# A decoder trunk on one core: the feed-forward layers' products go from rows of two into alternation of wide and narrow

## What is computed

```python
def conv_ffn(h, w_up, conv_w, conv_b, w_down):
    u = jnp.einsum('bsd,df->bsf', h, w_up)          # 2048 -> 11264
    S = u.shape[1]
    y = conv_b
    for tap in range(CONV_WIDTH):                   # 3
        shifted = jnp.pad(u, ((0, 0), (tap, 0), (0, 0)))[:, :S]
        y = y + shifted * conv_w[CONV_WIDTH - 1 - tap]
    val, gate = jnp.split(y, 2, axis=-1)
    return jnp.einsum('bsf,fd->bsd', jax.nn.silu(gate) * val, w_down)   # 5632 -> 2048

for l in range(DEPTH):                              # 2
    ...
    h = rms_norm(x, ffn_norm[l])
    x = x + conv_ffn(h, w_up[l], conv_w[l], conv_b[l], w_down[l]).astype(x.dtype)
```

## Time and profile before

| | |
|---|---|
| median of 3 runs | 1958.37 us (1958.27 to 1959.3) |
| the profiled execution's own time | 1958.57 us |
| its span, first to last instruction | 1956.4 us |
| TensorE busy | 1939.8 us (99%), 11078 products |
| VectorE, ScalarE busy | 1391.3 us (71%), 1110.1 us (57%) |
| granted TensorE clock | 0.998 of full |

### The profile page before, as it was taken

How to read it: one execution, slowest core, us unless ns; L and a number is a source line. 1 busy time by engine, 2 the same in 40 slices (tenths; PEclk the granted TensorE clock), 3 DMA queues, 4 the chain that set the end, 5 groups by cost and what they waited for, 6 DMA issues and landing times.

```text
span 1956.4 us, 31302 instructions
## 1 busy us (share of the span) xinstructions
PE 1939.8 (99%) x11078; PEld 1690.7 (86%) x11078; DVE 1391.3 (71%) x2152; ACT 1110.1 (57%) x1845; POOL 48.2 (2%) x53
## 2 busy tenths in 40 slices
PE   8999999999999999999999999999999999999998
PEld 8888888888888888888888888888888888888887
DVE  6667776767777777777655557877777777755554
ACT  6555554556665665665555456665665566545554
POOL 0002240000000000000000000000000000000000
PEclk9999999999999999999999999999999999999999
DMA  9654545555555555554565555555555555555653
GB/s 324 194 172 154 185 158 172 192 182 186 194 191 183 185 192 193 185 183 168 194 213 183 186 171 179 188 193 188 183 187 192 193 183 184 191 177 184 204 188 108
DMA packets 205202, 364.91 MB, mean 187 GB/s; under 512 B 6563, under 2 KB 49100, under 8 KB 205132
## 3 DMA queue, kind: packets, MB, share of 16 engines
q1 hardware_dynamic: 203388, 362.34, 55.9%
q10 hardware_dynamic: 1744, 1.63, 0.3%
HBM read 361.83 MB, written 2.11 MB: 186 GB/s over the span
## 4 chain that ended last, share of the span: by engine, by line
PE 97%; DVE 1%; ACT 0%; DMA 0%; issue 0%; DVEq 0%; SPq 0%
PE ps L389 53%; PE ps L392 26%; PE ps L447 7%; PE ps L451 3%; PE ps L481 2%; PE ps L484 2%; PE ps L483 2%; DVE lo L1095 1%; PE ps L465 0%; PE ps L467 0%; PE ps L468 0%; ACT hi L729 0%; PE ps L653 0%; PE ps L655 0%; PE ps L580 0%; PE ps L566 0%
## 5 line engine op out<-in xcount | busy, mean ns | idle before, releaser
L1095 DVE TENSOR_TENSOR lo<-raw,hi 128x512 fp32r<-128x512 f32 x1360 | 926.2, 697 | 520.3 <-ACT hi L729 516.1
L729 ACT ACTIVATE hi<-raw 128x512 fp32r<-128x512 f32 x1352 | 842.7, 630 | 791.4 <-PE ps L392 656.5
L389 PE MATMUL ps<-h,hi 128*128 128x512 f32 x2816 | 884.8, 396 | 0.0
L392 PEld LDWEIGHTS ps<-h,lo 128*128 128x128 f32 x2816 | 529.0, 188 | 125.1
L392 PE MATMUL ps<-h,lo 128*128 128x256 f32 x2816 | 553.2, 278 | 0.0
L389 PE MATMUL ps<-act,hi 128*128 128x512 f32 x1392 | 437.2, 395 | 0.0
L389 PEld LDWEIGHTS ps<-h,hi 128*128 128x128 f32 x2816 | 428.7, 189 | 0.3 <-DVE lo L1095 0.2
L392 PEld LDWEIGHTS ps<-act,lo 128*128 128x128 f32 x1392 | 261.5, 188 | 61.8
L392 PE MATMUL ps<-act,lo 128*128 128x256 f32 x1392 | 273.4, 278 | 0.0
L389 PEld LDWEIGHTS ps<-act,hi 128*128 128x128 f32 x1392 | 211.9, 189 | 0.0
L447 PE MATMUL ps<-h,hi 128*128 128x512 f32 x576 | 183.5, 400 | 0.9 <-DVE lo L1095 0.9
(11 more groups left out here) (183 smaller groups left out, 1106.9 us busy)
## 6 DMA issues: line engine op xcount, KB each, us to landing
raw<-in_w_up SPq DMA_DIRECT2D x176, 1024.0 KB, 5.0
raw<-in_w_down SPq DMA_DIRECT2D x88, 1024.0 KB, 5.1
raw<-in_w_in SPq DMA_DIRECT2D x54, 1024.0 KB, 5.2
raw<-in_w_out SPq DMA_DIRECT2D x16, 1024.0 KB, 5.1
raw<-in_pool_w SPq DMA_DIRECT2D x4, 1024.0 KB, 5.2
raw<-in_w_in SPq DMA_DIRECT2D x8, 256.0 KB, 4.6
x<-in_xT SPq DMA_DIRECT2D x8, 128.0 KB, 4.3
x<-in_xT SPq DMA_DIRECT2D x2, 512.0 KB, 7.4
```

The source lines that it names most:

```text
L389: pe.matmul(ps[:, bank + m, :], hi[:, kt, m * P:(m + 1) * P], mv, start=first and kt == 0, stop=False, skip_group_check=True)
L392: mm = pe.matmul(ps[:, bank + m, S:2 * S], lo[:, kt, m * P:(m + 1) * P], mv[:, 0:S], start=False, stop=last and kt == KT - 1, skip_group_c ...
L729: a_.activation(hi[:, kt, :], raw[:, slot, kt, :], ACT.Copy).then_inc(hi_done, 1)
L1095: ve.tensor_tensor(lo[:, kt, :], raw[:, slot, kt, :], hi[:, kt, :].bitcast(F32), ALU.subtract).then_inc(lo_done, 1)
```

## The change

`mixed_unit` takes the place of `wide_unit` in both feed-forward parts. It does the same products on the same operands into the same banks, in the order that a word of eight letters gives for each tile, and increments `w_used` on the tile's last product as before. Most tiles have the word WnWnWnWn; those of one column group (layer 0, down, group 1) have nWnWnWnW. The first pass of each up-projection stays in rows. Each column group opens with a word of its own: one or two tiles, one unit, or five units in rows, or a word between rows and alternation. By the words, of 1052 tiles that `mixed_unit` does 881 alternate throughout (841 and 40), 147 are in rows, and 24 are transitions. The down groups of layer 0 are now written out instead of looped over. `last_unit`, the output projection, the mixers and all other engines' programs are as before.

```diff
+            ROWS = "WWnnWWnn"
+            PAIRED = "WnWnWnWn"
+            NARROW_FIRST = "nWnWnWnW"
+
+            def mixed_unit(n, base, bank, first, moving, word, ready=None):
+
+                for kt in range(KT):
+                    pe.wait_ge(lo_done, base + KT * n + kt + 1)
+                    if ready is not None:
+                        ready(kt)
+                    mv = moving(kt)
+                    w = v = 0
+                    for kind in word(kt):
+                        if kind == "W":
+                            mm = pe.matmul(ps[:, bank + w, :], hi[:, kt, w * P:(w + 1) * P], mv,
+                                           start=first and kt == 0, stop=False, skip_group_check=True)
+                            w += 1
+                        else:
+                            mm = pe.matmul(ps[:, bank + v, S:2 * S], lo[:, kt, v * P:(v + 1) * P], mv[:, 0:S],
+                                           start=False, stop=False, skip_group_check=True)
+                            v += 1
+                    mm.then_inc(w_used, 1)
+
+            def up_word(l, gt, j):
+                if l == 0 and gt == 0:
+                    return lambda kt: ROWS if j == 0 and kt < 2 else PAIRED
+                if l == 0:
+                    return lambda kt: PAIRED if j or kt > 1 else ("WWnnWnWn" if kt else ROWS)
+                if gt == 0:
+                    return lambda kt: ROWS if j == 0 and kt == 0 else PAIRED
+                return lambda kt: "WnWWnnWn" if j == 0 and kt == 0 else PAIRED
+
+            def down_word(l, g, j):
+                if l == 0 and g == 0:
+                    return lambda kt: ROWS if j == 0 else PAIRED
+                if l == 0 and g == 1:
+                    return lambda kt: ROWS if j == 0 else NARROW_FIRST
+                if l == 0:
+                    return lambda kt: PAIRED if j or kt else ("WWWWnnnn" if g == 3 else "WWWnnnWn")
+                if g == 0:
+                    return lambda kt: PAIRED if kt else ROWS
+                if g == 1:
+                    return lambda kt: ROWS if j < 5 else PAIRED
+                if g == 2:
+                    return lambda kt: PAIRED if j or kt else "WWnWnnWn"
+                return lambda kt: ROWS if j == 0 else "WnWWnnWn" if j == 1 and kt == 0 else PAIRED
+
...
-                            wide_unit(U_UP[l] + 4 * gt + j, i * (8 * KT), wide_bank(G), j == 0, j == UP_UNITS - 1,
-                                      lambda kt: h[:, KT * j + kt, :], split if first and gt == 0 else None)
+                            mixed_unit(U_UP[l] + 4 * gt + j, i * (8 * KT), wide_bank(G), j == 0,
+                                       lambda kt: h[:, KT * j + kt, :], (lambda kt: ROWS) if first else up_word(l, gt, j),
+                                       split if first and gt == 0 else None)
...
-                def down(i, half, units):
-                    G = G_DN[l] + half
-                    pe.wait_ge(evacuated, i * 2 + G - 1)
-                    for j in range(units):
+                for g in range(DN_GROUPS):
+                    G = G_DN[l] + g
+                    pe.wait_ge(evacuated, G - 1)
+                    for j in range(DN_UNITS - (l == 1 and g == 3)):
                         pe.wait_ge(act_lo, l * PAIRS + j + 1)
-                        wide_unit(U_DN[l] + DN_UNITS * half + j, i * (2 * DN_UNITS * KT), wide_bank(G), j == 0,
-                                  j == DN_UNITS - 1, lambda kt: act[:, KT * j + kt, :])
-
-                if l == 0:
-                    with pe.Fori(0, DN_GROUPS // 2) as i:
-                        down(i, 0, DN_UNITS)
-                        down(i, 1, DN_UNITS)
-                else:
...
+                        mixed_unit(U_DN[l] + DN_UNITS * g + j, 0, wide_bank(G), j == 0,
+                                   lambda kt: act[:, KT * j + kt, :], down_word(l, g, j))
+            last_unit(U_DN[1] + DN_UNITS * DN_GROUPS - 1, wide_bank(G_DN[1] + 3))
```

## The result

The changed kernel takes 1971.45 us (median of three, 1970.73 to 1972.08) against 1958.37 us: 1.0065 times, with an interval of 1.0052 to 1.0078. It is **slower by 13 us**, where 1952.5 us was forecast. The profiled execution took 1970.73 us, its span 1968.6 us against 1956.4.

A forecast was written before the change was run, and what follows sets the result against it. TensorE, busy 99% of the span, was taken to bound the kernel by its products' pace; (a) gave -5.9 us, the rest nothing, so 1958.57 became 1952.7, less 0.2 for the median: 1952.5 us, range 1942 to 1968 us.

The forecast's parts named there:

- What bounds the kernel: Whole kernel: TensorE busy 99% of the span, so in the feed-forward parts only the products' own pace counts.
- (a): Order within a tile, feed-forward parts: 3524 pairs go from 348.3 to 346.7 ns, -5.9 us.
- (b): Openings of 40 loop and 8 down groups: some 10 ns each, 0.5 us, put at nothing.
- The last paragraph: What would show it: expected steps and counts, and ways to be wrong, such as an opening setting a group's slow pace.
- (c): Layer 0's down groups written out: loop or not costs nothing.
- (d): Waits hanging on `w_used`, still raised at the tile's end: 2.8 us of slack, untouched by a tile shorter by 0.007 us.
- (e): W and n of one block write the same bank in succession: no dearer than rows over changing banks.
- The slower one: Rival, every alternating tile: pairs settle at 350.0 to 352.5 ns, +5.9 to +14.7 us, 1964 to 1973 us; chance 0.28.
- changes of kind: Slower rival's argument: alternation switches wide to narrow and back twice as often, so 6.7 ns extra, 350.0 ns a pair.
- the second rival: No difference, alternating tiles: each product keeps its excess whatever its neighbours, 348.3 ns a pair, 1958 us; chance 0.16.
- The great gain: Rival, alternating tiles: loads finish better behind products, 344.2 to 341.7 ns a pair, -14.6 to -23.4 us; chance 0.22.
- The single-pair price: Last unit's four single W n pairs, 352.5 ns in the mean: +14.7 us if all alternating pairs cost that.

The follow-up runs named there:

- the last three runs: Tiles in rows two or three alternating tiles apart in the more-alternation kernel, and two apart in the kernel without openings; two apart on more alternation: 1954.5 us or below.
- the turning word: WnWWnnWn; as first tile of each loop group with `gt` 1 in the kernel without openings: 1961.09 us in one execution.
- the setting pair: The tiles WWnnWWnn WWnnWnWn; put with a later WnWWnnWn into the first pass of the kernel without openings: 1978.5 us.

## Why the prediction was wrong

*What bounds the kernel* was right: no wait entered the chain, the change showed in the products' pace alone, and its sum over pairs gives the new span to 0.1 us.

*(a) The price of an alternating pair.* The 346.7 ns that I took exist, to the tenth: they are the fast pace, and the kernel without openings took 1952.28 us where 1952.5 was forecast for the changed one. That agreement is in part luck. I had added 226.7 ns for a wide product alone and 120.0 for a narrow one alone; in the fast pace the wide step is 231.7 in the mean and the narrow one 115.0, so neither term holds and only their sum does. **The step that failed is the choice of one price for all 3524 pairs**: "a long alternation ... should settle at least as well as rows do". Alternation settles in either of two paces, and three quarters of the pairs settled at 353.3 ns. The four single pairs of the last unit, at 352.5, were near that pace. Whether they belong to it four pairs can't tell (from the starts in nanoseconds they are 356, 351, 350 and 352, not the slow cycle's 350, 361, 349), but they should have weighed as evidence that a dear pace exists; as a price for all pairs they gave +14.7 us, the nearest term to the measured +13.

*(b) The openings* I counted at 10 ns each, "at nothing beside the rounding". Their own length is indeed that small: with one tile in rows as every opening a fast group of sixteen tiles takes 22.19 us, which is 60 pairs at 346.7 ns and one tile at the rows' 1393 ns. But two readings were wrong. There are 58 openings and not 48, as layer 1's first down group opens each of its eleven units with a tile in rows. And the row that I took for the first full one behind other products was the second. The first took 0.80 us, from 1205.40 to 1206.20:

```profile
1205.40 0.73 PE L389 MATMUL ps<-h,hi 128*128 128x512 f32 x2
```

Neither moved the sum. What the openings did was to choose the pace of all that stands behind them up to the next opening: slow instead of fast costs 60 pairs x 6.67 ns = 0.4 us in a group of the up-projection and 172 x 6.67 = 1.15 us in one of the down-projection. The last paragraph named this case ("the opening word picks the one in which a group runs", "an opening put TensorE into a slow pace for the whole group") and gave it no chance and no price of its own.

*(c), (d) and (e)* held. Written-out code cost nothing (1959.64 us in one execution, the same span), TensorE waited for `lo` once, for 0.2 us, and the same bank twice running is in both paces, so it doesn't decide between them; what it costs by itself no run tells.

*The rivals.* The slower one (0.28, 1964 to 1973 us) has the sign and the size, with its mechanism half right: its settled dear pair is real, but it isn't the only one. Its reasoning by changes of kind (350.0 ns) fell, since one order has two prices, and so did the second rival's, a fixed excess for each product. What that excess over the streaming of the columns comes from no run shows, as every product here has a load of its own. The Trainium skill, page "TensorE: Matmul & The Clock Gate", section "Back-to-back issue gap", gives columns / 2.4 + 2.5 ns for a product by itself and says that in a stream of loads and products both set the spacing. The formula's 325 ns for a pair agree with neither pace here, 346.7 or 353.3. The great gain was not seen in any run.

*The range* ended at 1968 us with 0.12 left out above. The single-pair price lay outside it though it was the only row that showed the new order.

What is shown: the pace persists until the order is broken; openings change it; one tile in rows acts on the slow pace by where in its three-pair cycle it cuts, as the last three runs were built to test. For the turning word and the setting pair the same is read from the traces (20, 3, 18 and 1 cases) and was not tested by a run of its own. What stays open: why there are two paces at all; and what decides the pace at the first entry from rows, which differed between programs with the same words there (layer 1: fast without openings, slow with only the down groups' openings) and in one program between executions.

## What to carry to other kernels

When an engine never waits, the same instructions in the same order can still have two steady paces, so a short piece of a new order in the trace prices neither: look at long stretches, and count products in equal windows over the whole run. Where two paces exist, don't tune a break for each place; take the breaks out, or put two of them at the distance at which the second meets the step that turns slow into fast. Here that was two tiles in rows, two alternating tiles apart, at the entry, which gave 1951.88 us, 0.9966 times the kernel before, and fast layers in the trace, though no lower time than the kernel without any openings and its good entries (1952.28 us). And an entry that is good in one program isn't so in the next: check it again after each edit upstream, and in several executions, since one kernel here took 1965.6 to 1979.0 us with nothing changed between them.

## What the runs showed of the hardware

- Alternating fp32 products of 512 and 256 columns, each with its own load, settle at 346.7 or 353.3 ns a pair at a granted clock of 1.00; in rows of two every long stretch of the feed-forward parts ran at 348.3.
- The fast pace is not the sum of two settled streams: its wide steps are 231.7 ns in the mean and its narrow ones 115.0, against 226.7 and 120.0 for products of one width only.
- The slow pace repeats every three pairs (wide steps 233, 241, 236 ns), and it lasted for hundreds of microseconds, over loop edges and semaphore waits, in one case through all of layer 1's loop and down groups (1972 pairs).
- One order of eight products, WnWWnnWn, made the fast pace slow 21 times of 21; it made the slow one fast 20 times of 20 where it cut in at 233 or 241 and not once of three at 236.
- One tile in rows, WWnnWWnn, left the slow pace slow 44 times of 44 at 233 or 241 and made it fast four times of four at 236.
